# A hybrid decoder block on one core: the four x pieces as 512-column products, their halves added by VectorE

## The reference, cut to what matters

```
h = rmsnorm(x, norm_mix_w)
proj = h @ w_in                       # 1024 -> 3096 columns
q, k, v, g, a_low, z, xbc, dt_raw = split(proj)
conv = conv1d_causal(xbc, 4 taps)     # xbc: 1024 columns, the "x pieces"
...                                   # gated linear attention, SSD scan, output product
x = x + mixed @ w_out
x = x + moe_ffn(rmsnorm(x), ...)      # top 4 of 32 experts, clamped SwiGLU
return rmsnorm(x, final_norm_w)
```

## Time and profile before

| | |
|---|---|
| median of 3 runs | 3471.32 us (3469.68 to 3473.95) |
| the profiled execution, its own time | 3474.84 us |
| its span in the profile | 3473.2 us |
| TensorE (PE) busy | 3411.4 us, 98% |
| VectorE (DVE) busy | 2139.3 us, 62% |
| ScalarE (ACT) busy | 1607.8 us, 46% |
| GpSimd (POOL) busy | 637.0 us, 18% |

### The profile page before, as it was taken

How to read it: one execution, slowest core, us unless ns; L and a number is a source line. 1 busy time by engine, 2 the same in 40 slices (tenths; PEclk the granted TensorE clock), 3 DMA queues, 4 the chain that set the end, 5 groups by cost and what they waited for, 6 DMA issues and landing times.

```text
span 3473.2 us, 57451 instructions
## 1 busy us (share of the span) xinstructions
PE 3411.4 (98%) x21623; PEld 3107.6 (89%) x21623; DVE 2139.3 (62%) x2728; ACT 1607.8 (46%) x2047; POOL 637.0 (18%) x848
## 2 busy tenths in 40 slices
PE   7999999999999999999999999999999999999997
PEld 6888888888888999999999999988888888888986
DVE  3565355455456555655566666667777777777777
ACT  4443333333333444444444444455555555555555
POOL 1011111111113111111112111121112112212214
PEclk9999999999999999999999999999999999999998
DMA  9888888887875555555666666567666766776778
GB/s 373 327 311 328 303 286 302 301 291 278 300 275 176 165 174 175 175 175 183 184 197 195 198 185 193 189 211 233 224 209 215 237 226 223 245 230 223 246 240 318
DMA packets 475283, 826.58 MB, mean 238 GB/s; under 512 B 21838, under 2 KB 419294, under 8 KB 458785
## 3 DMA queue, kind: packets, MB, share of 16 engines
q1 hardware_dynamic: 443360, 721.83, 59.4%
q0 software_dynamic: 24320, 75.95, 9.6%
q10 hardware_dynamic: 7488, 27.27, 2.2%
HBM read 726.14 MB, written 98.96 MB: 238 GB/s over the span
## 4 chain that ended last, share of the span: by engine, by line
PE 92%; DMA 2%; DVE 2%; issue 1%; POOL 1%; ACT 1%; SPq 0%; POOLq 0%; DVEq 0%; ACTq 0%
PE pp L2039 14%; PE acc L2460 13%; PE acc L2456 10%; PE acc L2457 10%; PE acc L2458 10%; PE acc L2462 7%; PE pp L2029 5%; PE acc L2472 4%; PE acc L2474 4%; PE acc L2473 3%; PE tpm L2429 2%; PE tp L2008 2%; DMA uraw<-in_w_in 1%; PE tpm L2435 1%; PE seg L2084 1%
## 5 line engine op out<-in xcount | busy, mean ns | idle before, releaser
L1864 DVE TENSOR_TENSOR wlo<-raw,whi 128x2048 fp32r<-128x2048 f32 x384 | 876.0, 2289 | 301.5 <-ACT whi L1274 301.1
L1274 ACT ACTIVATE whi<-raw 128x2048 fp32r<-128x2048 f32 x384 | 730.1, 1910 | 151.7 <-PE acc L2474 103.0
L2460 PE MATMUL acc<-xhl,whi 128*128 128x512 f32 (+3 forms) x2304 | 762.9, 385 | 0.0
L680 POOL TENSOR_TENSOR gate_op<-gate_op 1x1 f32<-1x1 f32 x351 | 170.4, 485 | 2727.3 <-DVE ybuf L1902 532.4
L2462 PE MATMUL acc<-xhl,wlo 128*128 128x256 f32 (+3 forms) x2304 | 625.3, 271 | 0.0
L2456 PE MATMUL acc<-xhl,whi 128*128 128x272 f32 (+3 forms) x1792 | 535.6, 299 | 0.0
L2457 PE MATMUL acc<-xhl,whi 128*128 128x272 f32 (+3 forms) x1792 | 531.0, 296 | 0.0
L2458 PE MATMUL acc<-xhl,wlo 128*128 128x272 f32 (+3 forms) x1792 | 531.0, 296 | 0.0
L2460 PEld LDWEIGHTS acc<-xhl,whi 128*128 128x128 f32 x2304 | 432.3, 188 | 67.0
L1307 ACT ACTIVATE work<-acc,bgu 128x256 f32<-128x256 f32 (+7 forms) x400 | 173.0, 469 | 585.1 <-PE acc L2458 370.6
L2462 PEld LDWEIGHTS acc<-xhl,wlo 128*128 128x128 f32 x2304 | 438.7, 190 | 0.7
(11 more groups left out here) (330 smaller groups left out, 5726.2 us busy)
## 6 DMA issues: line engine op xcount, KB each, us to landing
u<-split_d SPq DMA_DIRECT2D x112, 2048.0 KB, 8.8
raw<-in_moe_w_gate SPq DMA_DIRECT2D x128, 1024.0 KB, 4.9
raw<-in_moe_w_up SPq DMA_DIRECT2D x128, 1024.0 KB, 4.9
raw<-in_moe_w_down SPq DMA_DIRECT2D x128, 1024.0 KB, 9.4
split_d<-u SPq DMA_DIRECT2D x16, 2048.0 KB, 13.5
uraw<-in_w_in SPq DMA_DIRECT2D x12, 1024.0 KB, 11.0
yT<-in_moe_b_down SPq DMA_DIRECT2D x18, 512.0 KB
xin<-in_x ACTq DMA_DIRECT2D x14, 512.0 KB, 9.3
```

The lines of the kernel that those rows point to most:

```text
L1274: act.activation(whi[:, q % RING, :, :], raw[:, q % RING, :, :], ACT.Copy).then_inc(a_hi, 1)
L1864: dve.tensor_tensor(wlo[:, q % RING, :, :], raw[:, q % RING, :, :], whi[:, q % RING, :, :].bitcast(F32), ALU.subtract).then_inc(v_lo, 1)
L2460: pe.matmul(into[:, 0:2 * n].rearrange("p (c n) -> p c n", c=2), hi_, of[:, k, :, 0:n], start=(k == 0), stop=False)
```

## The change

The high and low rows become one buffer, side by side (`hhl`). Each half c of a piece gets its own bank `pp[c]`: per step of k one matmul of 512 columns (high weights by high and low rows together) and one of 256 columns (low weights by high rows, added onto the second half of the bank). ScalarE copies the first 256 columns of the bank to `xT`, and VectorE then adds the last 256. The steps are named `x0a`, `x0`, ..., one for each half. Since every piece uses both banks, half c of piece n+1 waits for VectorE's sum of half c of piece n. `x_out(3)` moves ahead of `norm_sq` on ScalarE. `x_sum` is placed at four points of VectorE's order.

```diff
@@ x_out (ScalarE)
-                after(act, f"pe_x.x{n}", s)
-                copy(xT[:, 2 * n:2 * n + 2, TAPS - 1:], pair_cols(pp[n % 2][:, :], 2), f"act_x.x{n}")
+                for c, step in enumerate((f"x{n}a", f"x{n}")):
+                    after(act, "pe_x." + step, s)
+                    copy(xT[:, 2 * n + c, TAPS - 1:], pp[c][:, 0:PW], "act_x." + step)
@@ body (ScalarE)
                 if rec:
                     qk_out(b)
+                x_out(s, 3)
                 if tx:
...
                     norm_sq(a + 3)
-                x_out(s, 3)
                 if tx:
                     norm_xn(a + 3)
@@ new function (VectorE)
+            def x_sum(s, n):
+                for c, step in enumerate((f"x{n}a", f"x{n}")):
+                    after(dve, "act_x." + step, s)
+                    tt(xT[:, 2 * n + c, TAPS - 1:], xT[:, 2 * n + c, TAPS - 1:], pp[c][:, PW:], ALU.add, "dve_x." + step)
@@ body (VectorE)
                     mix_ssd(a - 2)
+                x_sum(s, 0)
                 if tx:
...
                     h_rows(a + 2, 0)
                 if rec:
                     ssd_add(a - 2)
+                x_sum(s, 1)
                 if post:
                     h2_T(q * 2, q * 2 + 1)
                 if split:
                     unit_lo(4)
                     unit_lo(5)
                 if rec:
                     qkv(b, 1, p)
                     gla_decay(b)
+                x_sum(s, 2)
+                if rec:
                     gla_add(b)
+                x_sum(s, 3)
                 dt_zb(s)
@@ x_piece (TensorE)
-                for c in range(2):
+                for c, step in enumerate((f"x{n}a", f"x{n}")):
+                    if free:
+                        after(pe, free[c], count)
+                    both = pp[c][:, :].rearrange("p (v n) -> p v n", v=2)
                     for k in range(KD):
-                        for w_, h_ in ((wh, hhi), (wh, hlo), (wl, hhi)):
-                            m = pe.matmul(pp[n % 2][:, c * PW:(c + 1) * PW], w_[:, k, c * P:(c + 1) * P], h_[:, k, :],
-                                          start=(k == 0 and w_ is wh and h_ is hhi), stop=(k == KD - 1 and w_ is wl))
-                done(m, f"pe_x.x{n}")
+                        pe.matmul(both, wh[:, k, c * P:(c + 1) * P], hhl[:, k, :, :], start=(k == 0), stop=False)
+                        m = pe.matmul(pp[c][:, PW:], wl[:, k, c * P:(c + 1) * P], hhl[:, k, 0, :],
+                                      start=False, stop=(k == KD - 1))
+                    done(m, "pe_x." + step)
@@ body (TensorE)
-                x_piece(s, 1, at)
+                x_piece(s, 1, at, ("dve_x.x0a", "dve_x.x0"), s)
-                after(pe, "act_x.x0", s)
-                x_piece(s, 2, at)
+                x_piece(s, 2, at, ("dve_x.x1a", "dve_x.x1"), s)
-                after(pe, "act_x.x1", s)
-                x_piece(s, 3, at)
+                x_piece(s, 3, at, ("dve_x.x2a", "dve_x.x2"), s)
```

More of the change, by code:

```diff
@@ L85 @@
     "act_sm": ["sm"],
-    "pe_x": ["x0", "x1", "x2", "x3"],
-    "act_x": ["x0", "x1", "x2", "x3"],
[3 rows of a table added]
     "pe_zz": ["zz", "tdt"],
@@ L194, in build @@
             hraw = pa("hraw", [KD, PW])
-            hhi = pa("hhi", [KD, PW], F32R)
-            hlo = pa("hlo", [KD, PW], F32R)
+            hhl = pa("hhl", [KD, 2, PW], F32R)
+            hhi, hlo = hhl[:, :, 0, :], hhl[:, :, 1, :]
             mT = pa("mT", [KD, P])
@@ L1672, in body @@
                     mix_ssd(b)
-                after(dve, "act_x.x3", s)
+                after(dve, "dve_x.x3", s)
                 if rec:
@@ L2020, in unit_of, with x_piece @@
                 return (u2[:, n % 4, c, :].rearrange("p (k n) -> p k n", k=k) for c in range(2))
-            def x_piece(s, n, at):
+            def x_piece(s, n, at, free, count):
                 ready(s, n, at)
                 wh, wl = unit_of(n, KD)
-                for c in range(2):
+                for c, step in enumerate((f"x{n}a", f"x{n}")):
+                    if free:
+                        after(pe, free[c], count)
+                    both = pp[c][:, :].rearrange("p (v n) -> p v n", v=2)
                     for k in range(KD):
-                        for w_, h_ in ((wh, hhi), (wh, hlo), (wl, hhi)):
-                            m = pe.matmul(pp[n % 2][:, c * PW:(c + 1) * PW], w_[:, k, c * P:(c + 1) * P], h_[:, k, :],
-                                          start=(k == 0 and w_ is wh and h_ is hhi), stop=(k == KD - 1 and w_ is wl))
-                done(m, f"pe_x.x{n}")
+                        pe.matmul(both, wh[:, k, c * P:(c + 1) * P], hhl[:, k, :, :], start=(k == 0), stop=False)
+                        m = pe.matmul(pp[c][:, PW:], wl[:, k, c * P:(c + 1) * P], hhl[:, k, 0, :],
+                                      start=False, stop=(k == KD - 1))
+                    done(m, "pe_x." + step)
             def rows_of_unit(n, t, th, tl):
@@ L2173, in body @@
                 after(pe, "dve_h.lo", s)
[L2174 to L2178, removed]
+                x_piece(s, 0, at, ("dve_x2.a1", "dve_x2.b1") if post else ("act_in.za", "act_in.zb") if rec else (),
+                        q if post else p)
                 if tx:
@@ L2218, in body @@
                 after(pe, "act_sm.sm", s)
-                after(pe, "act_x.x2", s)
+                after(pe, "dve_x.x3a", s)
                 for c in range(2):
@@ L2236, in body @@
                 after(pe, "dve_sp.zb", s)
-                first_half(s, 4, at, of_h, ("dve_sp.zb", "act_x.x3"), s)
+                first_half(s, 4, at, of_h, ("dve_sp.zb", "dve_x.x3"), s)
                 if rec:
```

## The result

| | before | changed |
|---|---|---|
| median of 20 runs | 3472.03 us (3469.24 to 3479.03) | 3478.36 us (3474.05 to 3485.85) |
| ratio | | 1.0019, 95% interval 1.0013 to 1.0025 |
| profiled execution, span | 3474.84 us, 3473.2 | 3478.56 us, 3477.0 |

The change costs 6.6 us by the ratio (4.5 to 8.7). That lies within the stated range of 3466 to 3481 us and, with an interval that reaches past it, just under the bound of 0.2%. But it is slower, and by more than the 2.6 us of the forecast.

The account below looks back on a forecast made before the run. TensorE bounds steady pairs, loads and splits of weights the first. First-pair delay 8.6 us minus matmul saving 6.0 gives +2.6 on 3471.32: 3473.9 us, range 3466 to 3481.

Parts of the forecast that it names:

- The mechanism: First pair: piece 3 waits for x_sum(2) behind unit_lo(5), idle some 11 us, starts at 59.25 us; decays near 98.
- copies and sums beneath the next half: Every pair: ScalarE's copies (0.6 us more) and VectorE's additions (3.4 us more) have slack; priced at nothing.
- The saving, 6.0 us: Matmuls of the pieces: 0.0129 us saved per step of k, 5.8 us over seven pairs plus 0.2 in the first.
- The first pair, 8.6 us: First pair: unit 4 starts at 70.0 us, against 61.4 to compare with; lasting delay 8.6 us (7.3 to 9.6).
- Piece 3 was to lose 3.0 us to the lower clock: First pair: after the idle stretch piece 3 runs 6.0 us at 1.2 GHz, losing 3.0 us (bounds 1.7 and 4.0).
- lost 1.7 us to the lower clock, which it no longer does, as the gap is now 1 us: Unit 4, first pair: its earlier 1.7 us clock loss disappears, so its 59.67 us start is compared as 61.4.
- Copies behind the DMA, priced at nothing: Piece 1 to 2: copies behind the second h2_of have 0.1 us to spare in the third pair, 3 in the sixth.
- the rival: Copies of piece 1 come late because the DMA behind h2_of lands later; at 4 us, 9 us more, 3483; chance 0.06.
- The first (the delay is taken up by the loads): Later loads absorb the first pair's delay: 3468.9 us if the 5.00 us stall is used up, 3465.3 if all; chance 0.13.
- Unit 6 did not wait for raw 7: First pair: rival that unit 6 waits for raw 7's load through unit_hi(7) and q's copy; up to 3480.4 us; chance 0.12.
- The rival on the matmuls' form: Matmuls of the pieces: the new form saves little, 1.2 us, so +7.4 us, 3478.7 us; chance 0.07.
- The move of x_out(3): ScalarE, x_out(3) ahead of norm_sq: delays norm_sq and norm_xn by 2 to 3 us, first reader some 25 us away; nothing.

Follow-up runs that it names:

- e4: Kernel before, with only one wait added: in the first pair piece 3 waits for unit_lo(5); ratio to the kernel before 1.0030.
- e1: Changed kernel with, in the first pair, x_out(3) ahead of unit_hi(5) on ScalarE and x_sum(2), x_sum(3) ahead of unit_lo(5) on VectorE; ratio to the kernel before 0.9999.
- e9: e7 with x_sum(2) also ahead of unit_lo(4) on VectorE in the first pair; ratio to the kernel before 0.9984.
- e5: Changed kernel with x_out(3) put back behind norm_sq on ScalarE; ratio to the kernel before 1.0055.
- e11: Changed kernel with 45 unit-matrix matmuls, into a bank nothing reads, ahead of piece 3 in the first pair; ratio to the kernel before 1.0017.
- e2: Changed kernel with x_out(1) between the two h2_of on ScalarE, so piece 1's copies don't wait for the second sum's DMA; ratio to the kernel before 1.0018.
- e3: Changed kernel with its banks, copies, sums and waits, but three matmuls of 256 columns per step of k; ratio to the kernel before 1.0032.
- e12: e9 with three matmuls of 256 columns per step of k; ratio to the kernel before 1.0001.
- e7: e6 with dt_zb also ahead of unit_lo(5) on VectorE in the first pair; ratio to the kernel before 0.9991.
- e8: Kernel before, without the change, with unit_hi(5) behind x_out(3) on ScalarE and unit_lo(5) behind dt_zb on VectorE; ratio to the kernel before 0.9992.
- e10: Changed kernel with 95 unit-matrix matmuls, into a bank nothing reads, ahead of piece 3 in the first pair; ratio to the kernel before 1.0037.
- e6: Changed kernel with the edits of e1 and e2 together; ratio to the kernel before 0.9999.

## Why the prediction was right, and where it was off

**The mechanism** was right in its main points. Piece 3 was foretold at 59.25 us and started at 59.12, behind 11.24 us released by VectorE; raw 7 at 67.9 and went at 66.43; `decays` near 98 and started at 97.54. e4 shows that this wait alone brings the cost, e1 and e9 that it goes away with the order. That copies and sums beneath the next half cost nothing held in the steady pairs; the wait of 1.33 us in the last pair was not foretold.

**The size** was off in the terms below; the forecast said 8.6 - 6.0 = 2.6 us, measured were 6.6 (4.5 to 8.7).

- *The saving, 6.0 us.* It was sized at 0.0129 us per step from the earlier trace rows. The steady pair measured 0.71 us, so 0.0111 us per step and 5.0 us over seven pairs. In piece 0 of the sixth pair the new steps are (651.10 - 646.16) / 14 = 0.3529 us apart, not the 0.3464 of the second stage. In piece 3 of e5's fourth pair they were (429.67 - 424.82) / 14 = 0.3464. What makes the difference between pieces is open. By the rule of the Trainium skill that the prediction weighed (TensorE: Matmul & The Clock Gate, "Back-to-back issue gap"), which the page gives for an isolated matmul, it would have been 0.0025 us; the rows don't agree with it for this pair of forms.
- *The first pair, 8.6 us.* Two steps on the clock missed, in opposite directions, and that the sum came out close is luck. Piece 3 was to lose 3.0 us to the lower clock (bounds 1.7 and 4.0). It took 66.33 - 59.12 = 7.2 us, against 5.8 us at full clock in e11, so it lost 1.4 us, and unit 4 started at 68.49 instead of 70.0. The other step is "lost 1.7 us to the lower clock, which it no longer does, as the gap is now 1 us": unit 4 ran at the lower level from 69 on. So there was nothing to take off, and its delay is the plain 68.49 - 59.67 = 8.8 us. e4 has 10.4 us for the wait in the whole (6.2 to 14.2), which takes in 8.6.
- *Copies behind the DMA, priced at nothing.* The waits were 0.3 us in the third pair, for which the prediction had 0.1 us to spare, and 1.3 us in the last, for which it took the 3 us of the sixth. Both come from a landing that was later than in the earlier trace rows, as the rival had it. e2 takes them away and is not measurably faster, so their share in the whole is not shown.

With the sizes as read in the profiles, and 8.4 us for the first pair at `decays`: 8.4 - 5.0 + 1.6 = 5.0 us, near the 5.5 us with which the second stage starts. With e4's 10.4 us it is 7.0. Both lie in the interval; which is nearer isn't settled.

**The rivals.** The first (the delay is taken up by the loads) did not come in the changed kernel's profile: `decays` waited 4.53 us instead of 5.00. It may come in part in other executions. In the profiles of e2, e3 and e5, whose first pair has the order of the change, `decays` waited 2.71, 2.58 and 2.50 us and started at 95.47, 96.40 and 95.20, so 6 to 7 us behind the earlier trace rows; in e4 it waited 6.04 and started at 98.25. There is one profile of the kernel before, so how much is taken up as a rule stays open. Unit 6 did not wait for raw 7: after the pause its load landed before ScalarE came to it, and the copy of q stood at 78.55 us. The rival on the matmuls' form was answered by the steady pairs of e3 and e12.

**The move of x_out(3)** was priced at nothing. As a cost that is right. What the prediction missed is what it covers: without it (e5) the change would have cost 19 us, not 6.6.

## What to carry to other kernels

Where a result moves from a copy by one engine to a copy and a sum by a second, list what stands ahead of the sum in the second engine's order in each written-out iteration, the first one above all: here one 2.3 us split of a unit that was still loading kept TensorE waiting for 11 us, and a new place in the order gave the cost back (1.0019 to 0.9999 in e1). Price a removed instruction by a mark that comes once per iteration, not by its distance within one row of matmuls: 0.71 us per pair was measured where 14 clean steps had said 0.83. Count for a wait of TensorE its length and look in the windows for the lower clock behind it: in e5 5.57 us of waiting brought another 5.5, while in e9 a wait of 0.95 us ahead of unit 4 brought none.

## What the runs showed of the hardware

- A gap was paid more than once. In e5 a wait of 5.57 us was followed by 12.98 us of busy time in windows at 0.50 to 0.69 of the clock, which lost 5.5 us more. The Trainium skill tells of such a loss after waits for DMA (TensorE: Matmul & The Clock Gate, "HAM oscillation — how this bites in real kernels"), and this trace agrees, with a wait for VectorE's sum in place of one for DMA.
- The level behind a gap is not the same each time. Ahead of unit 4 in the first pair TensorE waited 0.95 or 0.96 us in eleven of the profiles. In the changed kernel, e2, e3, e5 and e11 the lower level followed within 2 us; in e4, e7, e8, e9, e10 and e12 it did not. PE's window of e9 from unit 4 on:

```profile
56.00:83.00 27.00, 22.93 (x104) 1.00 1.01 418
```

- The stretch at the lower level around `decays` of the first pair ended near 97 us in the kernel before and near 106 in the changed kernel, some 10 us after it began in both. In e11, where `decays` started at 95.42 after a wait of 3.33 us instead of 5.00 and 4.53, it was over near 98.5, and the window that reads 0.53 in the changed kernel reads 0.87:

```profile
96.00:107.00 11.00, 11.00 (x44) 0.87 1.05 430
```

- Runs of one kernel differ by up to 13.5 us (e1), and the granted clock on record for each run goes with the time. Of the 17 runs of the kernel before beside e9 and e10 the fastest, 3468.34 us, had 0.995 and the slowest, 3480.25 us, 0.992; over all 17 the time falls by 3.1 us per 0.001 of the clock (correlation -0.89). Over the 20 runs of the changed kernel it falls by 3.6 us (-0.81). Over the 21 runs of the kernel before beside e11 and e12, which lie within 3.9 us, there is hardly a tie (-0.20). No run changed the clock alone, so that it is the cause is likely and not tested. A single profile can be off by as much: e6's profiled execution took 3467.59 us, its median is 3472.92.
- A matmul with float32 operands and 128 columns showed as two instructions and took 0.225 us (e10).
